# Sample streams' memory attention on 32-wide groups of columns of TensorE

## The reference

```
def mem_attention(q, mk, mv):
    bsz, l = q.shape[:2]
    s = jnp.einsum('bqhd,bmhd->bhqm', q, mk.astype(q.dtype)).astype(jnp.float32) * (1.0 / math.sqrt(MEM_HEAD_DIM))
    p = jax.nn.softmax(s, axis=-1)
    o = jnp.einsum('bhqm,bmhd->bqhd', p.astype(q.dtype), mv.astype(q.dtype))
    return o.reshape(bsz, l, MEM_WIDTH)
...
    m_out = mem_attention(mq.reshape(bsz, l, MEM_HEADS, MEM_HEAD_DIM), mk, mv) * jax.nn.silu(mg)
```

## Time and profile before

| | |
|---|---|
| runs | 2513.14, 2509.53, 2510.50 us; median 2510.5 |
| profiled execution | 2511.44 us, span 2509.7 us |
| mean granted TensorE clock | 0.971 of full |
| TensorE busy | 2396.4 us, 95% |
| VectorE, ScalarE, GpSimd busy | 42%, 36%, 16% |
| DMA | 293.38 MB, mean 117 GB/s |

### The profile page before, as it was taken

How to read it: one execution, slowest core, us unless ns; L and a number is a source line. 1 busy time by engine, 2 the same in 40 slices (tenths; PEclk the granted TensorE clock), 3 DMA queues, 4 the chain that set the end, 5 groups by cost and what they waited for, 6 DMA issues and landing times.

```text
span 2509.7 us, 35799 instructions
## 1 busy us (share of the span) xinstructions
PE 2396.4 (95%) x13821; PEld 2164.8 (86%) x13821; DVE 1046.3 (42%) x1688; ACT 892.5 (36%) x1635; POOL 407.1 (16%) x552
## 2 busy tenths in 40 slices
PE   8998998899899999999999999999999999989997
PEld 6798998899899998887788888989989898988886
DVE  5758878877642435223421221221212124423223
ACT  5532332233254334223322222454445454322221
POOL 1471452252101000001000000112121211000001
PEclk9999999999998899999999999999999999979999
DMA  7534343343534235223333334334343435334223
GB/s 261 193 91 105 83 105 87 76 105 88 173 118 132 89 107 176 76 75 110 109 97 96 117 96 124 123 98 138 101 142 99 128 114 210 100 97 151 76 75 134
DMA packets 197625, 293.38 MB, mean 117 GB/s; under 512 B 48324, under 2 KB 126672, under 8 KB 194096
## 3 DMA queue, kind: packets, MB, share of 16 engines
q1 hardware_dynamic: 117504, 154.16, 20.2%
q0 software_dynamic: 19856, 81.51, 10.1%
q10 hardware_dynamic: 60192, 56.69, 8.3%
HBM read 243.75 MB, written 48.55 MB: 116 GB/s over the span
## 4 chain that ended last, share of the span: by engine, by line
PE 78%; DVE 10%; issue 4%; DMA 4%; ACT 3%; ACTq 0%; POOL 0%; SPq 0%; DVEq 0%; POOLq 0%
PE PS L1255 10%; PE PS L1257 10%; PE PS L1256 10%; PE PS L206 10%; PE PS L208 10%; PE PS L207 10%; PE PS L815 2%; DVE WL L188 2%; DVE FA L617 1%; PE PS L1057 1%; DVE FA L618 1%; DVE FA L619 1%; PE PS L482 1%; DVE FA L622 1%; DVE FA L626 1%
## 5 line engine op out<-in xcount | busy, mean ns | idle before, releaser
L206 PE MATMUL PS<-XH,WH 128*128 128x320 f32 x2336 | 750.9, 321 | 26.1 <-DVE WL L188 22.4
L208 PE MATMUL PS<-XH,WL 128*128 128x320 f32 x2336 | 730.0, 312 | 0.0
L207 PE MATMUL PS<-XL,WH 128*128 128x320 f32 x2336 | 729.6, 312 | 0.0
L188 DVE SCALAR_TENSOR_TENSOR WL<-RAW,vec,WH 128x256 fp32r<-128x256 f32 (+1 forms) x608 | 355.6, 646 | 675.9 <-ACT WH L174 672.1
L206 PEld LDWEIGHTS PS<-XH,WH 128*128 128x128 f32 x2336 | 448.3, 192 | 34.4 <-DVE WL L188 24.8
L1255 PE MATMUL PS<-WH,XH 128*128 128x512 f32 x1168 | 461.9, 395 | 4.7 <-DVE WL L183 1.6
L1257 PE MATMUL PS<-WH,XL 128*128 128x512 f32 x1168 | 461.0, 395 | 0.0
L1256 PE MATMUL PS<-WL,XH 128*128 128x512 f32 x1168 | 460.5, 394 | 0.0
L207 PEld LDWEIGHTS PS<-XL,WH 128*128 128x128 f32 x2336 | 450.1, 193 | 3.1 <-issue 2.9
L208 PEld LDWEIGHTS PS<-XH,WL 128*128 128x128 f32 x2336 | 446.6, 191 | 0.0
L174 ACT ACTIVATE WH<-RAW,vec 128x256 fp32r<-128x256 f32 (+1 forms) x608 | 281.2, 532 | 460.5 <-DMA RAW<-in_w_kv_dram 181.4
(11 more groups left out here) (285 smaller groups left out, 2435.5 us busy)
## 6 DMA issues: line engine op xcount, KB each, us to landing
RAW<-in_w_in_a_dram SPq DMA_DIRECT2D x64, 512.0 KB, 4.0
RAW<-in_w_in_b_dram SPq DMA_DIRECT2D x64, 512.0 KB, 3.7
RAW<-in_w_kv_dram SPq DMA_DIRECT2D x48, 512.0 KB, 3.6
RAW<-in_w_out_a_dram SPq DMA_DIRECT2D x32, 512.0 KB, 3.8
RAW<-in_w_out_b_dram SPq DMA_DIRECT2D x32, 512.0 KB, 3.8
scratch_in_a<-EST ACTq DMA_DIRECT2D x32, 320.0 KB, 3.7
RAW<-in_w_glu_dram SPq DMA_DIRECT2D x24, 384.0 KB, 3.3
scratch_in_b<-EST ACTq DMA_DIRECT2D x26, 320.0 KB, 4.1
```

The source lines that it names most:

```text
L188: ins = eng.scalar_tensor_tensor(out=wview(WL, slot, ph)[:, kt, :], in0=wview(RAW, slot, ph)[:, kt, :], scalar=vec[:, g:g + 1], in1=wview( ...
L206: pe.matmul(acc, wh, xh, start=first, stop=False)
L207: pe.matmul(acc, wh, xl, start=False, stop=False)
L208: return pe.matmul(acc, wl, xh, start=False, stop=last)
```

## The change

The sample streams' two products change places of operands and are put on groups of 32 columns.
- A buffer QZ holds, for each parity a of a stream, head and pair m of streams, a stationary block of 32 columns: the stream's 16 queries in its half, zeros in the other. GpSimd clears QZ ahead of its first load; VectorE writes the queries by two copies (`mem_queries_dve`), in layer 1 too, where it now waits for the query load.
- s t becomes four products: QZ block stationary (32 columns), 256 turned key columns moving, output on partitions 32h to 32h+31. The two streams of a pair accumulate in one region. The rows are then (head, stream of the pair, query), the columns (pair, memory row).
- T 4 and its two copies are dropped. Softmax follows s 7 (slot 29) directly. P 4 moves from slot 33 to 32; V from slots 34 and 35 (three and five) to 33, 34 and 35 (two, three and three).
- MPT becomes half of PTZ, cleared by GpSimd ahead of V 0's load. P 4 is copied by two strided copies on each of ACT and VectorE, with zeros between.
- V t becomes eight products with 32-wide stationary blocks of PTZ, 128 value columns moving, output on partitions 32h to 32h+31 of bank 6.
- A step O 4 follows in slot 35, right behind V 7: ACT copies bank 6 to OV, TensorE turns it by four transposes into bank 7, VectorE gates it by four products.
- WL and RAW move from the end of the memory to right behind WH (offset 114816), all later buffers by 16 KB. The four semaphores of the first loads are shared with others.

```
-WL_AT = 208 * 1024 - 64
+WL_AT = 114816
...
-        WL = nc.alloc_sbuf_tensor_at("WL", [P, RING, 1024], F32R, offset=WL_AT)
+        WL = sb("WL", [P, RING, 1024], F32R)
...
-        s_memd = [sem(f"memory_quarter_loaded{k}") for k in range(4)]
+        s_memd = s_rowd[0:4]
...
-        MS, MROWS, MPR, MPT, sm = place([(MH, TOK), (5, 2, MEMW), (MH, NM), (2, MH, P), (2, 4, MH)])
+        MS, MROWS, MPR, sm, QZ, PTZ = place([(MH, TOK), (5, 2, MEMW), (MH, NM), (2, 4, MH), (2, MH, 4, 32), (2, 2, 4, MH * 32)])
+        MPT = PTZ[:, 0].rearrange("p a m c -> p (a m c)").rearrange("p (t h m) -> p t h m", t=2, h=MH)
+        OV = MPR[:].rearrange("p m k -> p (m k)")[:, 0:MEMW]
...
-                   (30, "T", 4), (33, "P", 4), (34, "V", 0), (34, "V", 1), (34, "V", 2), (35, "V", 3), (35, "V", 4),
-                   (35, "V", 5), (35, "V", 6), (35, "V", 7)]
+                   (32, "P", 4), (33, "V", 0), (33, "V", 1), (34, "V", 2), (34, "V", 3), (34, "V", 4), (35, "V", 5),
+                   (35, "V", 6), (35, "V", 7), (35, "O", 4)]
...
-                    for mt in range(2):
-                        for h in range(MH):
-                            ins = pe.matmul(stream_cols(PS[:, 4 + mt, h * P:h * P + P], t), KTM(t + 1)[:, h, mt * P:mt * P + P],
-                                            stream_cols(MQ[:, h, SEQ:TOK], t), start=(t == 0 and h == 0), stop=True,
-                                            skip_group_check=True)
+                        layer_wait(pe, l, "q_padded", 1)
+                    m, a = t // 2, t % 2
+                    for h in range(MH):
+                        ins = pe.matmul(PS[32 * h:32 * h + 32, 4 + m // 2, (m % 2) * NM:(m % 2 + 1) * NM], QZ[:, a, h, m, :],
+                                        KTM(t + 1)[:, h, :], start=(a == 0), stop=(a == 1), skip_group_check=True)
...
-                    for h in range(MH):
-                        for mt in range(2):
-                            ins = pe.matmul(stream_cols(PS[:, 6, h * P:h * P + P], t), MROWS[:, SLOT["V", t], mt, h * P:h * P + P],
-                                            stream_cols(MPT[:, mt, h, :], t),
-                                            start=(t == 0 and h == 0 and mt == 0), stop=(mt == 1), skip_group_check=True)
+                    m, a = t // 2, t % 2
+                    for mt in range(2):
+                        for h in range(MH):
+                            ins = pe.matmul(PS[32 * h:32 * h + 32, 6, m * P:m * P + P], PTZ[:, mt, a, m, 32 * h:32 * h + 32],
+                                            MROWS[:, SLOT["V", t], mt, h * P:h * P + P],
+                                            start=(a == 0 and mt == 0), stop=(a == 1 and mt == 1), skip_group_check=True)
                     ins.then_inc(mm["value_stream"], 1)
+                else:
+                    layer_wait(pe, l, "stream_copied", 1)
+                    for m in range(4):
+                        ins = pe.transpose(PS[:, 7, m * P:m * P + P], OV[:, m * P:m * P + P], ident[:])
+                    ins.then_inc(mm["stream_turned"], 1)
...
+            else:
+                layer_wait(dve, l, "q_loaded", 16)
+            layer_wait(dve, l, "zeros", 1)
+            for a in range(2):
+                src = MQ[:, :, SEQ:TOK].rearrange("p h (m a i) -> p h m a i", a=2, i=DSEQ)[:, :, :, a, :]
+                ins = dve.tensor_copy(QZ[:, a, :, :, DSEQ * a:DSEQ * a + DSEQ], src)
+            ins.then_inc(mm["q_padded"], 1)
...
+                        for a in range(2):
+                            ins = act.activation(padded(0)[a], streams(PS[:, 6, :])[:, a], ACT.Copy)
...
+                elif kind == "O":
+                    layer_wait(act, l, "value_stream", NB)
+                    act.activation(OV, PS[:, 6, :], ACT.Copy).then_inc(mm["stream_copied"], 1)
...
+            pool.memset(QZ[:], 0.0).then_inc(mm["zeros"], 1)
             for n, (kind, b, slot) in enumerate(ROWS):
...
+                if (kind, b) == ("V", 0):
+                    pool.memset(PTZ[:], 0.0).then_inc(mm["zeros"], 1)
```

More of the change, by code:

```diff
@@ L758, in mem_pe @@
                     n = TURN[kind, t]
-                    if n and TURNS[n - 1][0] != "s":
+                    if n:
                         mem_copied(pe, l, TURNS[n - 1])
@@ L839, in mem_queries_dve, with padded, streams @@
                 ins.then_inc(mm["q_ordered"], 1)
+                layer_wait(dve, l, "q_ordered", 1)
+            else:
[5 more added lines that the diff above has]
+            ins.then_inc(mm["q_padded"], 1)
+        def padded(mt):
+            v = PTZ[:, mt].rearrange("p a m c -> p (a m c)").rearrange("p (a x i) -> p a x i", a=2, i=DSEQ)
+            return [v[:, a, a::2, :] for a in range(2)]
+        def streams(v):
+            return v.rearrange("p (x a i) -> p a x i", a=2, i=DSEQ)
         def tile_of_banks(a):
@@ L868, in mem_act @@
                         layer_wait(act, l, "gate_ready", MH)
-                    act.activation(MPT[:, 0, :, :], tile_of_banks(6), ACT.Copy).then_inc(mm["high_copied"], 1)
+                    if t < NT - 1:
+                        act.activation(MPT[:, 0, :, :], tile_of_banks(6), ACT.Copy).then_inc(mm["high_copied"], 1)
+                    else:
+                        layer_wait(act, l, "zeros", 2)
+                        for a in range(2):
+                            ins = act.activation(padded(0)[a], streams(PS[:, 6, :])[:, a], ACT.Copy)
+                        ins.then_inc(mm["high_copied"], 1)
                     if t < NT - 2:
                         exps(t + 1)
[L872 to L875, removed]
+                elif (kind, t) == ("s", NB - 1):
+                    exps(NT - 1)
+                elif (kind, t) == ("S", 0):
                     exps(t)
+                elif kind == "O":
+                    layer_wait(act, l, "value_stream", NB)
+                    act.activation(OV, PS[:, 6, :], ACT.Copy).then_inc(mm["stream_copied"], 1)
         def mem_dve(dve, mine, l, unit):
@@ L916, in mem_dve @@
                         layer_wait(dve, l, "gate_ready", MH)
-                    dve.tensor_copy(MPT[:, 1, :, :], tile_of_banks(7)).then_inc(mm["low_copied"], 1)
+                    if t < NT - 1:
+                        dve.tensor_copy(MPT[:, 1, :, :], tile_of_banks(7)).then_inc(mm["low_copied"], 1)
+                    else:
+                        layer_wait(dve, l, "zeros", 2)
+                        for a in range(2):
+                            ins = dve.tensor_copy(padded(1)[a], streams(PS[:, 7, :])[:, a])
+                        ins.then_inc(mm["low_copied"], 1)
                     if t < NT - 2:
                         maxima(t + 1)
-                elif kind == "s" and t == NB - 1:
-                    layer_wait(dve, l, "values", NT - 1)
-                    dve.tensor_copy(MPT[:, 1, :, :], tile_of_banks(5)).then_inc(mm["low_copied"], 1)
-                elif kind == "T" or (kind, t) == ("S", 0):
+                elif (kind, t) == ("s", NB - 1):
+                    maxima(NT - 1)
+                    probs(NT - 1)
+                elif (kind, t) == ("S", 0):
                     maxima(t)
@@ L949, in mem_pool @@
                         layer_wait(pool, l, "turned", TURN[k, x] + 1)
+                    elif k == "s":
+                        layer_wait(pool, l, "scores", NT)
                     elif x < 0:
```

35 lines of the change are left out of this document (19 added, 16 removed).

## The result

The changed kernel takes **2445.2 us** (median of 4 runs, 2441.0 to 2446.7), the kernel before on the same chip 2510.0 (2509.4 to 2513.1): ratio 0.9737, interval [0.972, 0.9753]. The sign was right, the size was not.

A forecast was written before the change was run, and what follows sets the result against it. TensorE, busy 95% of the span, was taken as the bound; savings of 20.9, 20.7, 6.8 and 2.6 us against costs of 0.4, 2.7, 1.8 and 4.3 gave -41.8, from 2510.5 to 2469 us, range 2458 to 2491.

The forecast's parts named there:

- The move of WL: WL's new place next to WH: same instructions, no row prices an address, so 0 us.
- Value products: Value step of both layers: wider moving operands and column groups save 20.9 us in layer 0, 20.7 in layer 1.
- v: Time of one stream's value products after the change: 1.0 us, between 1.76 without overlap and 0.45 to 0.5 with four.
- Scores: Score step: a stream falls from 1.69 to 1.08 us; eleven of 16 gains of 0.62 survive, 6.8 us saved.
- The clock: Value step: the granted clock stays up with 128 moving columns; 2.4 us left for a low clock in layer 1.
- Rivals 3 and 4: Clock stays low in the values: without overlap 2525 us, chance 0.07; with pairs overlapping 2494 us, chance 0.06.
- V 7's load: Load for the last value stream: just hidden at 1.0 us a stream, 1 to 2 us late per layer with four overlapping.
- rival 2: Sample streams' products: four column groups run at once, values about 0.5 us a stream; -51.8 us, 2459 us, chance 0.14.
- Output transposes and glu: Behind the last value stream: transposes cost 1.35 us a layer, 2.7; glu's stall grows to about 2.3, costing 1.8.
- Value stretch in sum: From s 7 to the next projection, both layers: forecast terms together -40.5 us.
- The mode switches: Switches of TensorE's tiling mode around 22 column-tile stretches: taken as 0, up to 4.4 us kept for the range.
- The start: Start of each layer's attention: clearing QZ and padding queries cost 1.6 us in layer 0, 2.7 in layer 1, sum 4.3.

The follow-up runs named there:

- ring_back: The changed kernel with only the move of WL and RAW undone, back to the end of the memory: 2463.6 us, ratio 0.9813 to the kernel before.
- head_order: The changed kernel with the value product's loops exchanged, four records in a row to the same column group instead of two: 2444.2 us, ratio 0.9718.
- wide_moving: The kernel before with value products moving all 128 columns of probabilities instead of the stream's 16: 2490.7 us, ratio 0.9907.
- v_order: pad_late with V 2 one slot earlier, so three, two and three streams a slot: 2438.2 us, ratio 0.9707.
- one_group: The changed kernel with all four heads' sample-stream outputs on partitions 0 to 31, one column group: 2472.4 us, ratio 0.9839.
- pad_late: The changed kernel with QZ cleared behind the query and gate loads, and queries padded behind A 2 instead of ahead of S 0: 2439.2 us, ratio 0.9696.
- fills_late: v_order with layer 0's fills of k=1 and split of k=2 behind the P 4 copies on ScalarE and VectorE: 2434.8 us, ratio 0.970.
- ring_moved: The kernel before with only WL and RAW moved right behind WH, attention untouched: 2491.1 us, ratio 0.9932.
- before_aligned: The kernel before with WL at the end of the memory but 64 bytes lower, two small buffers cut to 24 columns: 2487.9 us, ratio 0.9906.
- ring_64_bytes: The changed kernel with WL next to WH but 64 bytes later, two small buffers cut to 24 columns: 2460.9 us, ratio 0.9802.
- ring_32_bytes: The changed kernel with a gap of 32 bytes ahead of WL, where ring_64_bytes had 64: 2461.2 us, ratio 0.9809.

## Why the prediction was wrong, step by step

**The move of WL, priced at 0.** "No row prices an address; 0" is the step that failed, and with it the range: the term measured 17 to 19 us by the two runs that move the ring alone. By the ratios the address is worth 16 to 24 us in the five kernels above, by the count of matmuls 18.7. Without it (ring_back) the changed kernel takes 2463.6 us, inside the range and 5 us from the forecast, and that nearness is partly luck: the next terms show that the attention gained more than forecast, and part of it was lost elsewhere in ring_back. A sign could be had from the trace before, though: 320 columns take 147.1 ns (23.10 us for 157), and 512 took 232.0. The difference is 0.442 ns a column; at 2.4 GHz a column is 0.417. Aligned it is (226.7 - 147.1)/192 = 0.415.

**Value products.** v was set to 1.0 between bounds of 0.45 and 1.76, and is 0.44: the mechanism "groups overlap" was right and the assumption of pairs was not. The forecast assumed that a product's second record, which follows the first on the same group, holds up the next head's first; head_order shows that it doesn't. 16 x 0.56 = 9.0 us more gained. On this the Trainium skill (TensorE: Matmul & The Clock Gate, Part 3) gives 2.38 times for three tiles; here four give four times, 0.110 to 0.0275 us a record, so the measurement goes beyond the page's figure.

**Scores.** Forecast 1.08 us a stream product, measured 0.57 on the chain. So each brings 1.12 instead of 0.62. Of 14 starts between s 0 and s 7 of both layers, 15.7 us could come; the stalls took 4.8 back: K 3's load 1.0 and 0.6 more, s 3 1.0 and 1.2, s 7 of layer 1 1.0. 10.9 stay, 11.2 are measured. The idea that stalls eat gains was right, and its count ("eleven left" of 16) near.

**The clock.** The assumption that it stays up was right in layer 0 (1.00), and the 2.4 us left for layer 1's low clock behind the stall became 5.4 us at 0.50, 2.7 lost. wide_moving shows that the old step's low clock came of its 16 moving columns (and as many written): nothing else differs. The old scores have 16 as well, and kept 1.00 over their 1.71 us, between projections. Rivals 3 and 4 are out.

**V 7's load.** I called it just hidden at v = 1.0, and 1 to 2 us late with four groups at once. It was 1.72 and 0.85, as rival 2 said; v_order shows that in layer 0 an earlier issue doesn't cure it.

**Output transposes and glu.** Forecast a stall of 0.9 ahead of the transposes: 0.71. Forecast 12.1 us of ScalarE between V 7's end and glu's start: 800.96 to 813.22, 12.3. The stall itself was forecast as 2.3 and is 0.56, only because TensorE was slowed to clock 0.84 and needed 10.6 us for what takes 8.8; where the clock stays up (one_group, pad_late, fills_late) it is 2.11.

**Value stretch in sum.** -40.5 forecast, 9.0 more by v, 1.0 more by the two s 7, 2.6 back for V 7: -47.9. Measured -47.0. The mode switches of the next paragraph, 0.3 us for each of six value stretches, take 1.9 off the 47.9; 1 us is left over, less than two executions of one kernel can differ.

**The mode switches.** They were taken at nothing, with 4.4 us kept for the range. The row behind that, an L206 of 0.41 us behind L494, doesn't show a switch: the starts of records do, and behind full-width float32 products an L206 lasts 0.39 as well. TensorE's timeline at such products (L801) in the changed kernel:

```profile
721.71 0.31 PE L208 MATMUL PS<-XH,WL 128*128 128x320 f32 x1
721.86 1.95 PE L801 MATMUL PS<-FA 128*128 128x128 f32 x16
723.56 0.39 PE L206 MATMUL PS<-XH,WH 128*128 128x320 f32 x1
723.79 0.31 PE L207 MATMUL PS<-XL,WH 128*128 128x320 f32 x1
```

L801 starts 0.15 us behind the last L208, the usual 0.147. Its 16 records of 0.112 and the next L206 would take 1.94, and they take 723.79 - 721.86 = 1.93. L810 starts 0.23 behind its L208 (793.88, 794.11), 0.09 late. Its 32 records of 0.0275 (0.88) take 1.01 until the next matmul starts (791.15, 792.16), 0.13 more, and the L206 behind a stretch takes 0.25 (795.56, 795.81), 0.10 more. Together that is 0.3 us a stretch of column tiles, the same in one_group, and 0.3 for the score stretches too: 6 to 7 us for 22 stretches, more than the 4.4. The score stretches' 0.14 within is already in the 0.57 above. The Trainium skill's rule that a change of the tiling mode drains TensorE (TensorEngine Tiling (Array Packing), Tiling Modes) agrees with this in its sign; it gives no price.

**The start.** +4.3 forecast, +4.1 in the two executions of the table. That match is luck in part. In layer 0 S 0 is only 0.7 later behind the first K transposes (8.11 us before, 8.84 after), in layer 1 0.9, not 2.7; the rest of the 4.1 is clock, 0.95 and 0.93 where the kernel before had 0.97 and 0.95. Over all traces here, six executions with the changed kernel's start take 64.5 to 66.2 and 67.5 to 70.0 us from the first K transpose to s 0, four with the start of the kernel before 63.6 to 65.7 and 67.7 to 68.5. Their means differ by 1.0 and 0.9. The three runs padded late are back at 63.7 to 64.9 and 67.8 to 68.1. In layer 0 one more part lies ahead of the window: GpSimd clears QZ (0.95 us) ahead of K 0's load, and the first K transposes wait for that load. That makes some 3 us, where the sum had 4.3.

**The chances.** Rival 2 had the mechanism in the attention: -51.8 forecast, -54.1 in the windows, -45.8 in ring_back's time. I gave it 0.14, for want of a row with two groups. No case had a gain outside the attention, so the range ended too early.

**Where the rest went.** The table has -12.1 us outside the attention, where the ring's place is worth 18.7. And the middle stretch took 1260.9 us in before but 1266.8 in ring_back, whose ring lies as before's does and whose instructions there are the same. Both are differences between executions. TensorE waits 2.83 us ahead of a block of small products (L1284 of before, L1329 with the change) and 2.2 us ahead of an earlier projection. Behind the first of these waits the granted clock stays at 1.00 in six of the thirteen traces here and is 0.53 to 0.71 in the others, up to the next projection matmul. Here are the block's line of the timeline and its window, in before and in ring_back:

```profile
1203.50 3.81 PE L1284 MATMUL PS<-FA 128*128 128x128 f32 x32 [2.83 <-DVE XL L1324]
...
1203.50:1207.31 3.81, 3.81 (x33) 1.00 0.67 276
```
```profile
1182.33 6.67 PE L1329 MATMUL PS<-FA 128*128 128x128 f32 x32 [2.83 <-DVE XL L1369]
...
1182.33:1189.00 6.67, 6.67 (x33) 0.55 0.40 160
```

That is 2.9 of the 5.9 us, and behind the other wait ring_back loses 1.6 more, at a clock of 0.78. The changed kernel's profiled execution has that block at 0.53 too, 2.9 us longer than at 1.00, and it was 2.2 us later at the start of the attention already (679.08 against 676.90), of which QZ's clearing explains 0.9. Together these are 5 of the 6.6 us that are missing from 18.7. Why the clock falls behind the same wait in one execution and not in the next stays open.

## What to carry to other kernels

Compare the cost a column of matmuls of two widths with the clock's: where the wide one is dearer, look at the address of what moves, before anything is rebuilt. Look at the granted clock of a stretch of narrow products even where TensorE is 100% busy: here it was 0.50, and a form that moves eight times the columns was faster even without overlap. When products get four times faster, price next what ran beside them: here the loads and the copies took back 4.8 us in the scores and the loads of V 2.6 in the values. And cut two or three executions of the same kernel at the same events before a difference of 2 us in one stretch is given a cause.

## What the runs showed of the hardware

- Three float32r matmuls of 512 columns, one of which moves the ring WL, take 680 ns where the ring starts on a multiple of 128 bytes (after, ring_moved, before_aligned), 696 at 64 bytes past it (before, ring_back, ring_64_bytes) and 693 at 32 (ring_32_bytes). Where the ring is the stationary operand, 320-column matmuls show no difference (147 ns in all).
- float32 products with a 32-column stationary on four column groups run four at a time: 0.110 us a record on one group, 0.0275 on four, in either order of issue. A stretch of them between full-width matmuls costs some 0.3 us more than its records.
- Products of 16 moving columns run at a granted clock of 0.69 over the first 48 records and of 0.50 over the later ones, with TensorE 100% busy; the same 128 with 128 moving columns keep 1.00 for 5.60 and 9.09 us.
- Of three 512 KB loads issued 0.72 us apart, the third took 6.62 us to land (v_order, layer 0); issued 0.85 us apart 4.93 (v_order, layer 1), and 2.3 us behind the second 5.09 (changed kernel).
